# Six small buffers in front of the weight ring, four behind the arena: every large tile at a multiple of 512 bytes

## The reference

```
for i in range(4):
    x = x + 0.5 * rms_norm(swiglu(rms_norm(x, g0), ff1_w_in[i], ff1_w_out[i]), g1)
    x = x + rms_norm(mixer(rms_norm(x, g2)), g3)     # attention, gated spatial MLP, differential attention, attention
    x = x + 0.5 * rms_norm(swiglu(rms_norm(x, g4), ff2_w_in[i], ff2_w_out[i]), g5)
```

```
x = x + (g_conv * y_conv + g_attn * y_nsa + g_mla * y_mla) @ w_out[l]
x = x + memory_cross_attention(rmsnorm(x), rmsnorm(mem), w_xq[l], w_xkv[l], w_xo[l])
x = x + (silu(gate) * up) @ w_down[l]
```

## The kernel before

| tile | before | after |
|---|---|---|
| ring and parts, x, hT, oT, xn, gain rows, o_rows, ident | 128 | 0 |
| gT | 320 | 0 |
| convwT | 320 | 0 |
| subln | 352 | 0 |
| tmp, sc | 128 | 0 |
| prT | 192 | 0 |
| hidden_high, hidden_low, arena | 192 | 0 |
| inside the arena: qz, kT, v_rows, merge gates (first parts) | 192 | 0 |
| inside the arena: vwin, qsz, kslcT, kwinT, vslc, glu, qnT, qpz, kpT | 4 | 0 |

## Time and profile before

### The profile page before, as it was taken

The page is one execution under the profiler, slowest core; times in us unless marked ns, Lnnn a source line. Parts: engine busy times, 40 slices in busy tenths (PEclk is TensorE's granted clock), DMA queues, the critical chain, the costliest instruction groups (busy, mean ns, idle before and its releaser), DMA issues.

```text
span 3040.3 us, 38290 instructions
## 1 busy us (share of the span) xinstructions
PE 2992.0 (98%) x15499; PEld 2526.9 (83%) x15499; DVE 1850.5 (61%) x2322; ACT 1480.4 (49%) x2163; POOL 84.1 (3%) x153
## 2 busy tenths in 40 slices
PE   8999999999999999999999999999999999999999
PEld 6889888888888888888888988897888889788887
DVE  5556655546655546755554665469775547977553
ACT  5445544435544435554443564354655434565542
POOL 0000000000000001000000000010000001000000
PEclk9999999999999999999999999999999999999999
DMA  7564455555555555265555635576244548615453
GB/s 229 186 208 141 161 192 177 194 190 199 183 181 190 190 181 186 84 201 188 193 180 175 219 119 193 179 203 210 84 159 150 190 166 226 200 69 171 152 189 126
DMA packets 302403, 532.98 MB, mean 175 GB/s; under 512 B 31074, under 2 KB 125204, under 8 KB 302228
## 3 DMA queue, kind: packets, MB, share of 16 engines
q1 hardware_dynamic: 288964, 511.63, 51.4%
q10 hardware_dynamic: 13264, 18.90, 1.8%
HBM read 528.33 MB, written 1.11 MB: 174 GB/s over the span
## 4 chain that ended last, share of the span: by engine, by line
PE 89%; DVE 8%; ACT 1%; issue 1%; DMA 1%; ACTq 0%; POOL 0%; SPq 0%; POOLq 0%; DVEq 0%
PE bank L724 85%; DVE sb_arena L2280 3%; DVE sb_parts L1819 2%; PE bank L1025 2%; PE bank L1053 1%; PE bank L805 1%; DMA sb_ring<-in_w_xq_dram 1%; ACT sb_parts L1321 0%; DVE sb_sc L2000 0%; PE bank L788 0%; PE bank L780 0%; ACT sb_sc L1457 0%; DVE sb_prT L2010 0%; POOL sb_rstd L1728 0%; DMA sb_ring<-in_ff_w_in_dram 0%
## 5 line engine op out<-in xcount | busy, mean ns | idle before, releaser
L1819 DVE TENSOR_TENSOR sb_parts<-sb_ring,sb_parts 128x2048 fp32r<-128x2048 f32 x480 | 1097.4, 2290 | 788.8 <-ACT sb_parts L1321 786.5
L724 PE MATMUL bank<-sb_parts,sb_hT_high 128*128 128x512 f32 (+1 forms) x4480 | 1370.0, 392 | 7.0 <-DVE sb_parts L1819 6.7
L1321 ACT ACTIVATE sb_parts<-sb_ring 128x2048 fp32r<-128x2048 f32 x480 | 914.5, 1913 | 790.6 <-PE bank L724 695.8
L724 PEld LDWEIGHTS bank<-sb_parts,sb_hT_high 128*128 128x128 f32 x4480 | 835.7, 188 | 184.4 <-DVE sb_parts L1819 11.0
L724 PE MATMUL bank<-sb_parts,sb_hT_low 128*128 128x512 f32 (+1 forms) x2240 | 853.0, 390 | 0.0
L724 PE MATMUL bank<-sb_parts,sb_hidden_high 128*128 128x512 f32 x1760 | 553.7, 395 | 0.0
L724 PEld LDWEIGHTS bank<-sb_parts,sb_hT_low 128*128 128x128 f32 x2240 | 420.9, 188 | 88.0
L724 PEld LDWEIGHTS bank<-sb_parts,sb_hidden_high 128*128 128x128 f32 x1760 | 328.3, 187 | 80.3 <-issue 0.6
L724 PE MATMUL bank<-sb_parts,sb_hidden_low 128*128 128x512 f32 x880 | 347.0, 394 | 0.0
L724 PE MATMUL bank<-sb_hT_high,sb_parts 128*128 128x256 f32 x1408 | 254.5, 283 | 0.0
L724 PEld LDWEIGHTS bank<-sb_hT_high,sb_parts 128*128 128x128 f32 x1408 | 220.1, 192 | 0.2
(11 more groups left out here) (220 smaller groups left out, 2083.8 us busy)
## 6 DMA issues: line engine op xcount, KB each, us to landing
sb_ring<-in_ff_w_in_dram SPq DMA_DIRECT2D x160, 1024.0 KB, 5.2
sb_ring<-in_ff_w_out_dram SPq DMA_DIRECT2D x88, 1024.0 KB, 4.9
sb_ring<-in_w_gate_up_dram SPq DMA_DIRECT2D x40, 1024.0 KB, 5.2
sb_ring<-in_w_in_dram SPq DMA_DIRECT2D x38, 1024.0 KB, 5.2
sb_ring<-in_a_w_qkv_dram SPq DMA_DIRECT2D x24, 1024.0 KB, 5.3
sb_ring<-in_w_down_dram SPq DMA_DIRECT2D x22, 1024.0 KB, 5.0
sb_ring<-in_ff_w_in_dram SPq DMA_DIRECT2D x32, 512.0 KB, 4.8
sb_ring<-in_c_w_qkv_dram SPq DMA_DIRECT2D x12, 1024.0 KB, 5.1
```

The source lines that it names most:

```text
L724: return nc.tensor.matmul(o, lhsT, rhs, start=start, stop=stop)
L1321: nc.scalar.activation(halves(n, slice(0, filled(n))).high, ring[:, raw_in[n], 0:filled(n)], ACT.Copy) \
L1819: V.tensor_tensor(both.low, ring[:, raw_in[n], 0:filled(n)], both.high.bitcast(F32), ALU.subtract) \
```

## The change

The order and the size of buffers change, and nothing else: no instruction is added, taken away or moved to another place in its engine's program, and no shape, semaphore or wait differs. Six small buffers (`fold` 128 bytes, `minus_half` 64, `mean_sq` 64, `rstd` 64, `lam` 32, `ssum` 32: together 384) are allocated in front of the ring, which therefore begins at 16,896, a multiple of 512. Four others (`valid`, `stats`, `moments`, `nmax`) go behind the arena. In the arena 47 floats are left free in front of `vwin`.

```diff
+        fold = sb("fold", [P, 2, CMP_STRIDE])
+        minus_half = sb("minus_half", [P, 16])
+        mean_sq = sb("mean_sq", [P, 16])
+        rstd = sb("rstd", [P, 16])
+        lam = sb("lam", [P, 8])
+        ssum = sb("ssum", [P, 8])
+
         with nc.sbuf_tensor("sb_parts", [P, RING, SLOT], F32R) as parts_of:
             ring_parts = parts_of
         ring = sb("ring", [P, RING, SLOT])
@@
         ident = sb("ident", [P, P])
-        fold = sb("fold", [P, 2, CMP_STRIDE])
-        minus_half = sb("minus_half", [P, 16])
         gT = sb("gT", [P, 3, P])
         convwT = sb("convwT", [P, 2, P])
-        lam = sb("lam", [P, 8])
         subln = sb("subln", [P, P])
         cosb = sb("cosb", [P, NT, 32])
         sinb = sb("sinb", [P, NT, 32])
-        valid = sb("valid", [P, NT])
-        ssum = sb("ssum", [P, 8])
-        mean_sq = sb("mean_sq", [P, 16])
-        rstd = sb("rstd", [P, 16])
-        stats = sb("stats", [P, 2, 6])
-        moments = sb("moments", [P, NT, 2])
         tmp = sb("tmp", [P, 512])
         sc = sb("sc", [P, 3, 2 * S])
-        nmax = sb("nmax", [P, 3, 4])
         prT = sb("prT", [P, 2, 2 * S])
@@
         arena = sb("arena", [P, AR])
+        valid = sb("valid", [P, NT])
+        stats = sb("stats", [P, 2, 6])
+        moments = sb("moments", [P, NT, 2])
+        nmax = sb("nmax", [P, 3, 4])
         used = [0]
@@
         w2v = part(2 * DH, "p (f d) -> p f d", f=2)
-        here = used[0]
+        used[0] = -(-used[0] // P) * P
         vwin = part(NT * P, "p (t n) -> p t n", t=NT)
```

## The result

The changed kernel takes 3023.1 us in the median of six runs (3022.42 to 3025.75) against 3043.22 us for the kernel before. The ratio is 0.9935, with a 95% interval of 0.9925 to 0.9944, so 17 to 23 us less. The forecast was 2900 us with a range of 2855 to 3030: the time lies inside the range, but less than a sixth of the forecast saving came. Rival B had 3024 us.

A forecast was written before the change was run, and what follows sets the result against it. TensorE's cost per matmul was taken to bound the kernel. Savings of 107.7 and 45.7 us, together 153.4, less 11.3 lost, gave net 142.1 us off 3042.0: 2900 us, range 2855 to 3030.

The forecast's parts named there:

- Rival B: fp32r matmuls: 32 cycles are fixed, only hidden's 16 more come from the address; 17.6 us less, 3024 us, chance 0.20.
- What bounds the kernel: Whole kernel: TensorE has a matmul in flight for 2992.0 of 3040.3 us, so only the cost of one matmul can change.
- The step that failed: Loaded fp32r blocks: each float past a 512-byte boundary costs one cycle, so starting at 0 saves 32 or 48 cycles.
- the 216 ns of the sum: 512-column fp32r matmuls with aligned blocks: assumed pace, including a small rest of 2.7 ns.
- its upper bound: All fp32r matmuls: with no rest left, the saving would be 187 us.
- The term of 107.7 us: Matmuls loading from hT, oT or the ring's parts: 10,068 times 10.7 ns saved.
- The term of 45.7 us: Matmuls loading from hidden: 2,640 times 17.3 ns saved.
- The 11.3 us of loss: Convolution's stretches, where VectorE leads the chain of waits: saving of 1,053 fp32r matmuls at 10.7 ns counted as lost.
- Rivals C and D: C: addresses don't matter, 3042 us, chance 0.12. D: blocks starting at a multiple of 256 cost more, 3194 us, chance 0.08.
- The parts costed at 0: Ring's feed, VectorE operations and taps, small buffers, and the arena gap with attention's plain float32: each taken as 0 us.
- The ring's feed: Chunks must come 0.26 us sooner (hidden 0.42); ScalarE's slack of 1.45 us each covers it, so 0 us.
- ScalarE's waits for TensorE should shrink: Sign expected in the new trace: ScalarE waits less than 695.8 us for ring slots, without TensorE waiting for low parts.

## Why the prediction was wrong

*What bounds the kernel* was read rightly: what moved is TensorE's pace, its busy time fell by 16.2 us, and a pace times a count, 17.6 us, lies in the measured interval. The counts and the two paces of the earlier trace rows held too.

*The step that failed* is the reading of those paces: "a block of 512 bytes which straddles a 512-byte boundary costs as many cycles more as it has floats on the far side", and with it "If the line goes on to 0, a matmul loses its 32 or 48 cycles". The pace is no function of the loaded block's own start: blocks at 0, 64 and 128 have 226.7 to 226.9 ns in step with the ring, and a block at 0 has 232.4 out of step. In the kernel before, hT and ring happened to share their distance, so own start and distance to the ring could not be told apart, and that the 32 and 48 cycles equal 128/4 and 192/4 floats was a coincidence. No run shows the 216 ns of the sum, nor the 213.3 ns of its upper bound, an estimate of 512 columns at 0.4167 ns each with nothing over: with 512 columns the lowest mean of 24 matmuls in a row is 226.6 ns, over the traces of all runs. The term of 107.7 us for hT, oT and the ring's blocks measured 0, as all were in step already. The term of 45.7 us for hidden measured 17.6: 6.67 ns each and not 17.3. The 11.3 us of loss in the convolution's stretches fell away with the saving there.

*Rival B* had the size right for this reason: 3024 us, from "16 more". It named two causes. The first, a start that is no multiple of 128 bytes, is refuted by the kernel with everything 64 bytes off; the second, unlike distances of loaded and streamed block, is what the runs show, though modulo 256 and not 512. I gave it 0.20 because "two causes" seemed dearer than one line, and because the streamed starts of the 472-column chunk made no difference among themselves. That reading of the earlier trace rows was right and the conclusion from it wrong: at 472 columns the distance does not show at all, as the kernel with the ring at 64 confirms, and at 512 it does. The same rows had a warning that I passed over: 40 cycles over the width of 472 don't fit the 32 over 256 and 512. They stay without an account.

*Rivals C and D* fall with hidden's 226.7 ns: addresses do matter, and a multiple of 512 is not the dearest place. A hidden block as little as 16 bytes out of step took 231.9 or 234.8 ns and not 226.7.

*The parts costed at 0* stayed there: all that the change does beside hidden's distance to the ring differs by 1.8 us from hidden alone put into step, 3021.09 against 3022.89 us in the same comparison, with intervals that overlap. Attention's period moved by the view's 10 ns. That float32 is deaf to addresses was argued from the tiles' own starts, 4 and 192 bytes behind a multiple of 512, with 2.19 us a period at both. Of the products timed there only those with the values had operands at unlike distances, and they too kept their pace, as shown above. The ring's feed held, from the changed kernel's page:

```profile
L1322 ACT ACTIVATE sb_parts<-sb_ring 128x2048 fp32r<-128x2048 f32 x480 | 914.8, 1914 | 771.2 <-PE bank L725 700.8
```

ScalarE still waited 700.8 us for TensorE before its high parts, so it stayed ahead. "ScalarE's waits for TensorE should shrink" did not come true, with 695.8 before. But the test was easier than planned, with 0.16 us less per chunk on hidden and none elsewhere.

What the remaining 32 cycles are stays open. They are not the loaded floats and not a fixed cost (230.0 ns with fewer columns, 117.8 instead of 120.0 ns with 256 columns out of step). In step they are the same at 256 and 512 columns because the unit is taken from these two widths; out of step the pace varies with D, and at 472 columns, 213.3 to 214.0 ns, the same unit leaves 40 to 42. Why the distance should count modulo 256 bytes is not settled either; the runs show that it does, with 226.8 ns for hidden at D = 256 and 232.4 at 128.

## What to carry to other kernels

Where fp32r matmuls of 512 columns follow each other back to back, put the loaded and the streamed tile at the same distance from a multiple of 256 bytes; here it was worth 3% of each matmul, 226.7 instead of 233.3 ns, and whether that distance is 0 did not matter (226.8 ns with all at 64, 226.9 at 128). With 256 columns (120.0 ns in step, 116.7 at D = 224) and with 472 (214.0 ns either way) it was not so here, and other widths were not tried: read the pace from start to start in your own trace. A law fitted through as many points as it has parameters is no law: before trusting one, look for a second variable that moved along with the first, here the ring's own start, and give the plain reading of the pair its due. And a residue in a case too small to matter for the time, here the 40 cycles at 472 columns, can still contradict the law.

## What the runs showed of the hardware that was not expected

- The pace of an fp32r matmul depends on the distance between what is loaded and what streams: with 512 columns, loaded from hT or hidden, 226.7 ns in step and 232.4 to 235.8 ns in the means at the distances tried (4 to 144 bytes), modulo 256 (226.8 ns for hidden at D = 256). With 472 columns, rows 1,888 bytes apart, it is 214.0 ns both with one start of four in step and with none. Plain float32 matmuls showed no such thing where their distance changed: eight products with the values, 64 columns each, take 0.84 us at D = 188 and at 0.
- With 256 columns, loaded from the ring, some distances are faster than none: 120.0 ns in step, 116.7 at D = 224, 117.8 at 192, and 120.0 again at 160. A layout with the wide products in step and the narrow ones out of it was not tried; by 2,424 x 2.2 to 3.3 ns it would be worth an estimated 5 to 8 us.
- Loading 64 or 96 columns instead of 128 makes the matmul slower, 230.0 against 226.7 ns (one run).
